# Softmax mixers and indexer in blocks of 16 meta tokens and 128 tokens, a search for the 16 lowest scores in the short block, and keys and indexer first in the weight stream

## The chip, the cores and the metric

The kernel runs on one core of one Trainium2 chip. The metric is the device time of one execution in microseconds (us), where lower is better. The kernel before takes 1382.4 us (median of 3 runs, 1382.38 to 1383.15).

## The reference, cut to what matters

The reference is two layers of a decoder trunk with D = 1024. 16 learned meta tokens stand ahead of 512 tokens, and are dropped at the end. All is in float32. A layer is

```
a    = rms_norm(h)
proj = a @ w_in                      # columns: dq dk dv iq iw ik | fq fk fv ff | gq gk gv gg lr
# DSA: 4 heads, one shared key; an indexer with 4 heads picks the keys of each query
score = sum_h iw[q,h] * relu(iq[q,h] . ik[k]) / 8, admissible keys only (k <= q)
sel   = top_k(score, 128)            # ties go to the earlier key
o_a   = softmax over sel of (rope(norm(dq)) . rope(norm(dk)) / 8) @ dv
# FoX: 4 heads, softmax attention with a forget gate (cumulated log-sigmoid) in the logits
# GLA: 4 heads, gated linear attention in chunks, RMS norm and SiLU gate on its output
h = h + concat(o_a, o_b, o_c) @ w_out
h = h + (silu(f @ w_gate) * (f @ w_up)) @ w_down,   f = rms_norm(h)
```

A query picks 128 keys. Among the first 144 tokens (16 meta tokens and 128 tokens) at most 16 keys are left out.

## The kernel before, in words

**Weights.** All weights come as a stream of units of 128 output columns by 1024 rows, 100 loads for each layer: 24 of the input projection, 8 of the output projection, 44 of gate and up, 24 of down. SyncE loads a unit into one of two buffers `raw` (L697), ScalarE rounds it to `whi` (L1187, "round"), GpSimd takes the rest `wlo = raw - whi` (L727, "split"), and TensorE multiplies with three products of the parts (whi x xhi, whi x xlo, wlo x xhi). Unit n+2 can be rounded only when TensorE is done with unit n. `DQ, DKIK, IQ, SMALL, FQ, ...` (top of the file) give each unit its number in the stream: units 0 and 1 are the queries of DSA, 2 is its key together with the indexer's key, 3 and 4 are the indexer's queries, 5 (`SMALL`) holds dv, the indexer's weights iw and the small gates.

**Tokens.** 528 tokens are 5 blocks of BLK = 106 (`NB`), 530 with two padded. Softmax mixers, indexer and GLA all use these blocks. A DSA or FoX head of block i works on (i + 1) * 106 keys: `logits` (TensorE L1012, then VectorE L1607: mask, negate and minimum in one pass, then ScalarE L1337: exp), `turn` (TensorE transposes L1021, ScalarE copy L1345), `values` (TensorE L1035), and for 4 heads together `scale` (VectorE L1618, L1619), `back` (TensorE L1044) and `mixed` (ScalarE L1376, VectorE L1628), which write the block's part of the output projection's input. The ten groups of four heads go in `ATTEND_ORDER`, which begins with the two groups of block 0. Both layers do all ten.

**The choice of keys.** For blocks 1 to 4 the indexer computes `index` (TensorE L992, ScalarE relu L1328, VectorE weighted sum L1571 and L1573, and after the fourth head the causal mask L1578). Then `topk` runs 16 rounds on VectorE, each one MAX8 (the 8 largest, L1585) and a match and replace (two instructions, L1586) over all keys of the block; `select` (L1591, L1592) turns the marks into a mask. The DSA logits of block i wait for it. The first `index` on TensorE waits for all five rotary units (`ROPE_ORDER`), the copies of the keys and `clear_keys` on GpSimd.

**GLA and the end of the mixers.** GLA's output is normed, gated and split on VectorE and ScalarE (L1666, L1671, L1381, L1676). `out` part 0 multiplies the GLA half of the first output units once all four `gla_lo` (L1676) are there; part 1 adds the attention half once the last `mixed` is done. After that the rest of the layer, which is output projection and FFN, is one long stream of units.

**The order of the work.** In the projection and mixer stage a planner (`plan`, `work`) writes out one static order for each engine. It has a cost table for each step, what each step waits for, and a list of priorities for each chain of steps (`BIAS`, one dict per layer). It fills TensorE between mixer steps with thirds of projection units. Each engine then runs its list in order. A step that waits holds up what stands behind it on that engine. In layer 1 the units made for queries only are computed for the 512 tokens alone. A layer's first two units go ahead of the list in `first_halves`.

Of the kernel before, what the change touches and what calls it, by code (L numbers as in the profile page):

```python
# [15 lines left out]
NB = 5  # L16
# [5 lines left out]
CUT = NT // 2  # L22
KT = D // 128
FF = 2816
MF = FF // 128
TOPK = 128
# [6 lines left out]
DQ, DKIK, IQ, SMALL, FQ, FK, FV, GQ, GK, GV, GG = 0, 2, 3, 5, 6, 8, 10, 12, 14, 16, 20  # L33
# [16 lines left out]
C_TRI = C_CAU + BLK  # L50
# [14 lines left out]
NORMED = {0: P_DQ, 1: P_DQ, 2: P_DK, 6: P_FQ, 7: P_FQ, 8: P_FK, 9: P_FK}  # L65
ROPED = (0, 1, 2, 3, 4)
# [3 lines left out]
ATTEND_ORDER = [(0, 0), (1, 0), (0, 1), (1, 4), (0, 2), (1, 3), (0, 3), (1, 2), (0, 4), (1, 1)]  # L70

# [33 lines left out]

HEADS = [(g, i, h) for g, i in ATTEND_ORDER for h in range(4)]
NORM_ORDER = [DQ, DQ + 1, DKIK, FQ, FQ + 1, FK, FK + 1] + [GV + h for h in range(4)]
ROPE_ORDER = (DKIK, DQ, DQ + 1, IQ, IQ + 1)
# [5 lines left out]
def chains_of_steps(l):  # L114

    choose = []
    for i in range(1, NB):
        choose += [("topk", i, r) for r in range(TOPK // 8)] + [("select", i)]
# [8 lines left out]
        "index": [("index", i, h) for i in range(1, NB) for h in range(4)],  # L127
# [10 lines left out]
        "logits": [("logits", *h) for h in HEADS],  # L138
        "turn": [("turn", *h) for h in HEADS],
        "values": [("values", *h) for h in HEADS],  # L140
        "scale": [("scale", *a) for a in ATTEND_ORDER],
        "back": [("back", *a) for a in ATTEND_ORDER],
        "mixed": [("mixed", *a) for a in ATTEND_ORDER],
# [7 lines left out]
def work(l, step):  # L151
# [4 lines left out]
    if kind in ("index", "topk", "select"):  # L156
        keys = (a[0] + 1) * BLK
    elif kind in ("logits", "turn", "values"):
        keys = (a[1] + 1) * BLK
# [60 lines left out]
    if kind == "clear_keys":  # L220
        return [(POOLE, 2.1, [(("proj", 3, 1, PIECES - 1), POOLE)])]
# [12 lines left out]
    if kind == "index":  # L234
        i, h = a
        n = 4 * (i - 1) + h
        cut = [min(keys, 512)] + ([keys - 512] if keys > 512 else [])
        used = [(("index", (n - 2) // 4 + 1, (n - 2) % 4), DVEE)] if n >= 2 else []
        return [(PE, sum(pe_fp32(c) for c in cut), ropes + [(("copies",), ACTE), (("clear_keys",), POOLE)]),
                (ACTE, act_us(keys, True), used),  # L240
                (DVEE, dve_us(keys, h > 0) + (0.3 if h == 3 else 0),
                 [turned(SMALL)] + ([(("logits", 0, i - 2, 3), DVEE)] if i >= 3 else []))]
    if kind == "topk":
        return [(DVEE, 0.46 + keys / 480, [(("index", a[0], 3), DVEE)])]
    if kind == "select":
        i = a[0]
        return [(DVEE, 0.6 + keys / 960, [])]
    if kind == "logits":
        g, i, h = a
        u = HEADS.index(a)  # L250
# [3 lines left out]
        before = [(("turn", *HEADS[u - 3]), PE)] if u >= 3 else []  # L254
# [3 lines left out]
    if kind == "turn":  # L258
        u = HEADS.index(a)
        return [(PE, 0.091 * (a[1] + 1), [(("logits", *a), ACTE)]),  # L260
                (ACTE, act_us(keys, True), [(("values", *HEADS[u - 2]), PE)] if u >= 2 else [])]
    if kind == "values":
        g, i, h = a
        n = ATTEND_ORDER.index((g, i))
        return [(PE, 0.186 * (i + 1), [(("turn", *a), ACTE)] + [turned(t) for t in ((FV, FV + 1) if g else (SMALL,))] +
                 ([(("scale", *ATTEND_ORDER[n - 1]), DVEE)] if h == 0 and n else []))]
    if kind == "scale":
        n = ATTEND_ORDER.index(a)
        return [(DVEE, 0.62, [(("values", *a, 3), PE)] + ([(("back", *ATTEND_ORDER[n - 1]), PE)] if n else []))]
# [25 lines left out]
    if kind == "out":  # L295
        if a[0] == 0:
            return [(PE, 4.4, [(("gla_lo", h), DVEE) for h in range(4)] + [evicted(N_PROJ - 1)])]
        return [(PE, 1.5, [(("mixed", *x), DVEE) for x in ATTEND_ORDER])]
# [10 lines left out]
def width_of(job):  # L309
    block = job[1] if job[0] == "index" else job[2] if job[0] in ("logits", "turn") else 0  # L310
    return 2 if job[0] in WIDE_KINDS or (block + 1) * BLK > 512 else 1
# [44 lines left out]
def tails(l, chains):  # L356
# [33 lines left out]
    for key in ops:  # L390
# [4 lines left out]
BIAS = ({'gla_lo': -60.8, 'prenorm': -39.5, 'turn': 91.9, 'gla_att': -2.6, 'norm': 26.4, 'gla_out': 147.1, 'mixed': -2.9, 'square': 15.1, 'gate': 4.2, 'fox': -28.5, 'out': 1.3, 'index': -23.6, 'gla_mix': -64.4, 'silu': -26.6, 'choose': -112.9, 'back': 49.6, 'proj': -40.9, 'scale': 56.4, 'gla_kv': -4.2, 'values': -16.4, 'turn_tile': -5.1},  # L395
        {'gla_lo': -34.5, 'prenorm': 40.0, 'copies': 16.5, 'clears': -85.6, 'gla_att': -2.9, 'logits': -10.1, 'norm': 78.2, 'gla_out': 174.3, 'mixed': 55.0, 'square': 5.1, 'gate': 5.6, 'fox': 6.6, 'out': -170.7, 'index': -19.4, 'gla_mix': -47.0, 'silu': 68.1, 'choose': -52.0, 'back': -18.0, 'proj': -38.1, 'rope': 4.4, 'scale': 82.1, 'turn_tile': 34.1, 'values': 8.4})
# [3 lines left out]
def plan(l, bias=None, start=9.0):  # L400
# [5 lines left out]
    info, drains = {}, {("back",) + a: [(("spread_sums",), POOLE)] + [(("gate", t), PE) for t in range(2)] for a in ATTEND_ORDER}  # L406
# [82 lines left out]
LOGITS = {s: n for n, s in enumerate(HEADS)}  # L489
GROUPS = {s: n for n, s in enumerate(ATTEND_ORDER)}  # L490
BACKS = GROUPS
ROPES = {k: n for n, k in enumerate(ROPE_ORDER)}
INDEX = {(i, h): 4 * (i - 1) + h for i in range(1, NB) for h in range(4)}
# [58 lines left out]
def hybrid_block(nc, hT, weights, params, consts, out):  # L552
    with ExitStack() as ctx:
# [18 lines left out]
        with ExitStack() as mixers:  # L572
# [1255 lines left out]
```

## Time and profile before

| | |
|---|---|
| median of 3 runs | 1382.4 us |
| the profiled execution's own time | 1382.82 us |
| its span in the profile | 1381.0 us |
| TensorE (PE) busy | 1356.4 us, 98% |
| VectorE (DVE) busy | 672.1 us, 49% |
| ScalarE (ACT) busy | 503.4 us, 36% |
| GpSimd (POOL) busy | 531.8 us, 39% |
| DMA | 112.46 MB, mean 81 GB/s |

The page gives an engine's busy time as the union of its instructions. TensorE's matmuls overlap, and their ends are modelled, so a gap on TensorE is a little longer than the profile shows it. The mixer stage of layer 0 is about 14 to 271 us, that of layer 1 about 715 to 961 us. The rest is the output projection and the FFN.

### The profile page before, as it was taken

What the parts mean: (1) busy time and instruction counts of PE and PEld (TensorE: products, weight loads), DVE (VectorE), ACT (ScalarE), POOL (GpSimd) and SP (SyncE); (2) the same over time, 40 slices, a digit from 0 to 9 for tenths busy, and PEclk for the clock granted to TensorE, in tenths of its full rate; (3) what the DMA queues carried; (4) which work ended last, traced back from release to release, by engine and by line L of the source; (5) the groups of instructions that cost most, each with busy time, mean ns of one, the idle gap of its engine ahead of it and who ended that gap; (6) DMA issues with size and microseconds to landing.
All of it is one profiled execution on the core that took longest, in us unless ns stands there. A gap on an engine that the chain in (4) does not pass through costs nothing.

```text
span 1381.0 us, 23323 instructions
## 1 busy us (share of the span) xinstructions
PE 1356.4 (98%) x8908; PEld 1221.5 (88%) x8908; DVE 672.1 (49%) x1174; ACT 503.4 (36%) x745; POOL 531.8 (39%) x248
## 2 busy tenths in 40 slices
PE   7999999999999999999999999999999999999998
PEld 7999889899999999999988988787878888888887
DVE  4669888654333333322235789895543333332000
ACT  5344545533222222322233553446332232223122
POOL 2553110243444444444436532111444444444444
PEclk9999999999999999999999999999999999999999
DMA  4221100122222222223222121011222332223234
GB/s 182 77 77 62 48 31 1 62 76 92 87 84 88 90 91 91 92 92 107 91 83 86 63 76 47 17 47 31 77 92 91 96 101 91 91 91 107 96 102 152
DMA packets 32170, 112.46 MB, mean 81 GB/s; under 512 B 3696, under 2 KB 4080, under 8 KB 31984
## 3 DMA queue, kind: packets, MB, share of 16 engines
q1 hardware_dynamic: 31392, 110.58, 24.3%
q10 hardware_dynamic: 720, 1.09, 0.2%
q8 instruction: 39, 0.64, 0.2%
q14 instruction: 19, 0.16, 0.0%
HBM read 109.55 MB, written 2.10 MB: 81 GB/s over the span
## 4 chain that ended last, share of the span: by engine, by line
PE 57%; issue 30%; POOL 8%; DVE 4%; ACT 1%; POOLq 0%; DMA 0%; SPq 0%; DVEq 0%; ACTq 0%
PE ps L837 19%; PE ps L843 9%; POOL wlo L727 8%; PE ps L933 5%; PE ps L927 5%; PE ps L928 5%; PE ps L1012 2%; PE ps L1035 2%; PE ps L941 1%; PE ps L992 1%; PE ps L1021 1%; PE ps L968 1%; DVE feat L1552 1%; PE ps L951 1%; PE ps L1076 1%
## 5 line engine op out<-in xcount | busy, mean ns | idle before, releaser
L727 POOL TENSOR_TENSOR wlo<-raw,whi 128x1024 fp32r<-128x1024 f32 x202 | 501.1, 2481 | 832.1 <-ACT whi L1187 831.9
L1187 ACT ACTIVATE whi<-raw 128x1024 fp32r<-128x1024 f32 x202 | 213.7, 1058 | 597.0 <-PE ps L843 559.9
L837 PE MATMUL ps<-xhi,whi 128*128 128x264 f32 (+1 forms) x1088 | 327.2, 323 | 7.2 <-ACT whi L1187 7.1
L837 PE MATMUL ps<-xlo,whi 128*128 128x264 f32 (+1 forms) x1088 | 325.7, 323 | 0.0
L837 PEld LDWEIGHTS ps<-xhi,whi 128*128 128x128 f32 x1088 | 205.3, 189 | 24.8 <-ACT whi L1187 6.8
L837 PEld LDWEIGHTS ps<-xlo,whi 128*128 128x128 f32 x1088 | 205.2, 189 | 16.4
L843 PE MATMUL ps<-xhi,wlo 128*128 128x264 f32 (+1 forms) x1088 | 195.3, 322 | 0.4 <-POOL wlo L727 0.2
L927 PE MATMUL ps<-xhi,whi 128*128 128x264 f32 (+1 forms) x640 | 181.7, 314 | 1.0 <-DVE feat L1473 1.0
L843 PEld LDWEIGHTS ps<-xhi,wlo 128*128 128x128 f32 x1088 | 162.4, 188 | 17.7 <-issue 1.0
L928 PE MATMUL ps<-xlo,whi 128*128 128x264 f32 (+1 forms) x640 | 171.8, 298 | 0.0
L837 PE MATMUL ps<-hhi,whi 128*128 128x264 f32 (+1 forms) x528 | 157.0, 320 | 0.0
L837 PE MATMUL ps<-hlo,whi 128*128 128x264 f32 (+1 forms) x528 | 156.9, 320 | 0.0
L1704 DVE TENSOR_TENSOR hid<-ps,rstd 128x528 f32<-128x528 f32 (+1 forms) x44 | 30.8, 700 | 213.1 <-PE ps L843 213.1
L927 PEld LDWEIGHTS ps<-xhi,whi 128*128 128x128 f32 x640 | 120.6, 188 | 6.7 <-DVE feat L1473 1.2
L928 PEld LDWEIGHTS ps<-xlo,whi 128*128 128x128 f32 x640 | 120.7, 189 | 4.7 <-issue 0.7
L1719 DVE TENSOR_TENSOR h<-ps,h 128x528 f32<-128x528 f32 (+1 forms) x16 | 11.2, 700 | 204.1 <-PE ps L843 204.1
L837 PEld LDWEIGHTS ps<-hhi,whi 128*128 128x128 f32 x528 | 99.3, 188 | 7.7
L837 PEld LDWEIGHTS ps<-hlo,whi 128*128 128x128 f32 x528 | 99.2, 188 | 7.6
L933 PE MATMUL ps<-xhi,wlo 128*128 128x264 f32 (+1 forms) x640 | 105.0, 306 | 0.3 <-POOL wlo L727 0.3
L1710 DVE TENSOR_TENSOR hlo<-hid,hhi 128x528 f32 (+1 forms) x44 | 82.9, 1885 | 41.0 <-ACT hhi L1410 41.0
L843 PE MATMUL ps<-hhi,wlo 128*128 128x264 f32 (+1 forms) x528 | 95.6, 321 | 0.0
L933 PEld LDWEIGHTS ps<-xhi,wlo 128*128 128x128 f32 x640 | 88.2, 188 | 5.3 <-issue 1.0
(154 smaller groups left out, 1742.0 us busy)
## 6 DMA issues: line engine op xcount, KB each, us to landing
raw<-in_weights SPq DMA_DIRECT2D x202, 512.0 KB, 3.5
out_hT<-h SPq DMA_DIRECT2D x8, 256.0 KB, 4.3
h<-in_hT SPq DMA_DIRECT2D x4, 264.0 KB, 6.3
h<-in_hT ACTq DMA_DIRECT2D x4, 264.0 KB, 5.8
cst<-in_consts SPq DMA_DIRECT2D x1, 1035.0 KB, 9.7
par_all<-in_params SPq DMA_DIRECT2D x1, 144.0 KB, 9.4
par_all<-in_params SPq DMA_DIRECT2D x1, 140.0 KB, 9.5
cst<-in_consts SPq DMA_DIRECT2D x1, 128.0 KB, 4.8
```

Of the source, the lines that this page charges most:

```text
L727: nc.gpsimd.tensor_tensor(wlo[:, b], raw[:, b], whi[:, b].bitcast(F32), ALU.subtract).then_inc(split_done, 1)
L837: nc.tensor.matmul(bank(bank_no, cut.stop - cut.start), whi[:, b, k % KT], x(k)[t][:, cut], start=(first and k == ks[0] and t == 0), stop= ...
L843: ins = nc.tensor.matmul(bank(bank_no, cut.stop - cut.start), wlo[:, b, k % KT], x(k)[0][:, cut], start=False, stop=(last and k == ks[-1]))
L927: nc.tensor.matmul(o, whi[:, k % 2, n], xhi[:, n, cut], start=(n == 0), stop=False)
L928: nc.tensor.matmul(o, whi[:, k % 2, n], xlo[:, n, cut], start=False, stop=False)
L933: ins = nc.tensor.matmul(o, wlo[:, k % 2, n], xhi[:, n, cut], start=False, stop=(n == KT - 1))
L941: ins = nc.tensor.matmul(bank(b0 + hf, HALF), lhs, sqb[:, SQUARES[k] % 2, hf * HALF:(hf + 1) * HALF], start=True, stop=True)
L1012: ins = nc.tensor.matmul(ps[0:BLK, b0 * 512 + a:b0 * 512 + z], q, key[:, a:z], start=True, stop=True)
L1035: ins = nc.tensor.matmul(ps[0:BLK, 3 * 512 + hd * 65:3 * 512 + (hd + 1) * 65], probs_t[:, u % 2, j, :], v, start=(j == 0), stop=(j == i))
L1187: return nc.scalar.activation(whi[:, b], raw[:, b], ACT.Copy).then_inc(hi_done, 1)
L1704: nc.vector.tensor_tensor(tokens(l, hid[:, b]), wide(l, 4 * b + 2), tokens(l, rstd[:]), ALU.mult).then_inc(ev.acc_free, 1)
L1710: nc.vector.tensor_tensor(hlo[:, bass.ds(j * 2 + b, 1), of].rearrange("p a t -> p (a t)"), hid[:, b, of], hhi[:, bass.ds(j * 2 + b, 1), of ...
```

## The change

It does five things.

1. The softmax mixers and the indexer take query blocks and key blocks of 16 meta tokens (block 0) and then 128 tokens each (blocks 1 to 4), with 16, 144, 272, 400 and 528 keys. GLA keeps its blocks of 106.
2. In the last layer the two attention groups of block 0, the meta tokens' queries, are left out, as the output drops them.
3. Block 1, with 144 keys, does not look for the 128 highest scores. The scores are negated with the causal mask in the same instruction, and `lowest` finds the 16 highest of these (MAX8, match and replace, MAX8). `select` then marks the scores at the sixteenth value or beyond and treats ties by a running count. The mask has the same meaning as before.
4. The stream begins with the keys (DKIK), the indexer's queries (IQ) and SMALL, and the DSA queries (DQ) follow as units 4 and 5. The first `index` waits for three rotary units, not five; `clear_keys` on GpSimd may come after unit 1, not unit 3; VectorE's first weighted sum waits for `masks` on GpSimd. In layer 1 `first_halves` takes three halves (both of DKIK, and IQ).
5. The planner's costs and its priorities `BIAS` are new, so all engines' lists in the mixer stage are new.

```
-DQ, DKIK, IQ, SMALL, FQ, FK, FV, GQ, GK, GV, GG = 0, 2, 3, 5, 6, 8, 10, 12, 14, 16, 20
+DKIK, IQ, SMALL, DQ, FQ, FK, FV, GQ, GK, GV, GG = 0, 1, 3, 4, 6, 8, 10, 12, 14, 16, 20
+QB = 128
+NQ = 1 + SEQ // QB
+def keys_to(i):
+    return META + QB * i
+def tokens_of(i):
+    return slice(keys_to(i - 1) if i else 0, keys_to(i))
+def rows_of(i):
+    return slice(0, QB if i else META)
-HEADS = [(g, i, h) for g, i in ATTEND_ORDER for h in range(4)]
-ROPE_ORDER = (DKIK, DQ, DQ + 1, IQ, IQ + 1)
+ATTENDED = [[(g, i) for g, i in ATTEND_ORDER if i or l < DEPTH - 1] for l in range(DEPTH)]
+HEADS = [[(g, i, h) for g, i in ATTENDED[l] for h in range(4)] for l in range(DEPTH)]
+ROPE_ORDER = (DKIK, IQ, IQ + 1, DQ, DQ + 1)
+INDEX_ROPES = 3
...
-    for i in range(1, NB):
-        choose += [("topk", i, r) for r in range(TOPK // 8)] + [("select", i)]
+    for i in range(1, NQ):
+        choose += [("lowest", i)] if keys_to(i) - TOPK <= 16 else [("topk", i, r) for r in range(TOPK // 8)]
+        choose += [("select", i)]
...
     if kind == "clear_keys":
-        return [(POOLE, 2.1, [(("proj", 3, 1, PIECES - 1), POOLE)])]
+        return [(POOLE, 2.1, [(("proj", 1, 1, PIECES - 1), POOLE)])]
...
                 def first_halves():
-                    halves_now = proj_halves(l)[:2]
+                    halves_now = proj_halves(l)[:3 if l else 2]
...
                 def index(i, hd):            # TensorE
-                        pe.wait_ge(ev.roped, len(ROPES))
+                        pe.wait_ge(ev.roped, INDEX_ROPES)
...
                 def index(i, hd):            # VectorE
                     if n == 0:
...
+                        dve.wait_ge(ev.masks_ready, 5)
...
-                    if hd == 3:
+                    if hd == 3 and nk - TOPK <= 16:
+                        chain(nc.vector.scalar_tensor_tensor(sc, sc, -1.0, causal_to(nk), ALU.mult, ALU.subtract))
+                    elif hd == 3:
...
+                def lowest(i):
+                    nk = keys_to(i)
+                    sc, rest = score[:, i % 2, 0:nk], score[:, i % 2, nk:2 * nk]
+                    chain(nc.vector.max(top8[:, 0:8], sc))
+                    chain(nc.vector.match_replace(out=rest, in_to_replace=top8[:, 0:8], in_values=sc, imm_value=TAKEN))
+                    chain(nc.vector.max(top8[:, 8:16], rest))
                 def select(i):
+                    if nk - TOPK <= 16:
+                        eq, cum = score[:, i % 2, nk:2 * nk], score[:, i % 2, 2 * nk:3 * nk]
+                        edge, among = top8[:, nk - TOPK - 1:nk - TOPK], top8[:, 16:17]
+                        chain(nc.vector.tensor_scalar(eq, sc, edge, None, ALU.is_equal))
+                        chain(nc.vector.tensor_tensor_scan(cum, eq, eq, 0.0, ALU.add, ALU.max))
+                        same = score[:, i % 2, 3 * nk:4 * nk - TOPK]
+                        chain(nc.vector.tensor_scalar(same, top8[:, 0:nk - TOPK], edge, None, ALU.is_equal))
+                        chain(nc.vector.tensor_reduce(among, same, AX.X, ALU.add))
+                        chain(nc.vector.tensor_tensor(among, cum[:, nk - 1:nk], among, ALU.subtract))
+                        chain(nc.vector.scalar_tensor_tensor(cum, cum, among, eq, ALU.is_gt, ALU.mult))
+                        chain(nc.vector.scalar_tensor_tensor(sc, sc, edge, cum, ALU.is_gt, ALU.add))
+                        nc.vector.scalar_tensor_tensor(sc, sc, NEG, causal_to(nk), ALU.mult, ALU.add).then_inc(ev.selected, 1)
...
                 def values(g, i, hd):
                     for j in range(i + 1):
-                        v = v_dsa[:, j] if g == 0 else v_fox[:, j, hd]
-                        ins = nc.tensor.matmul(ps[0:BLK, 3 * 512 + hd * 65:3 * 512 + (hd + 1) * 65],
-                                               probs_t[:, u % 2, j, :], v, start=(j == 0), stop=(j == i))
+                        keys, queries = rows_of(j), rows_of(i)
+                        v = v_dsa[keys, j] if g == 0 else v_fox[keys, j, hd]
+                        ins = nc.tensor.matmul(ps[queries, 3 * 512 + hd * 65:3 * 512 + (hd + 1) * 65],
+                                               probs_t[keys, u % 2, j, queries], v, start=(j == 0), stop=(j == i))
```

## Rows read from the trace of the kernel before

**Rows 1.** The page: busy time by engine.
```profile
PE 1356.4 (98%) x8908; PEld 1221.5 (88%) x8908; DVE 672.1 (49%) x1174; ACT 503.4 (36%) x745; POOL 531.8 (39%) x248
```

**Rows 2.** Busy time by stage: stretch, length, PE, PEld, DVE, ACT, POOL busy, granted clock, DMA.
```profile
14.00:85.00 71.00, 70.85 (x526) 68.12 (x525) 36.65 (x50) 28.12 (x41) 37.05 (x29) 1.00 0.22 75
85.00:250.00 165.00, 161.99 (x1263) 148.07 (x1262) 147.08 (x378) 82.14 (x152) 35.09 (x15) 1.00 0.14 45
250.00:271.00 21.00, 18.01 (x137) 14.63 (x136) 14.83 (x34) 13.82 (x27) 5.09 (x2) 0.99 0.17 58
271.00:290.00 19.00, 19.00 (x147) 19.00 (x147) 7.94 (x9) 4.55 (x7) 4.80 (x2) 0.92 0.16 49
715.00:760.00 45.00, 43.41 (x235) 37.05 (x235) 23.94 (x29) 17.94 (x25) 23.50 (x18) 1.00 0.21 71
760.00:941.00 181.00, 177.73 (x1242) 156.59 (x1241) 154.14 (x379) 89.65 (x164) 46.48 (x26) 1.00 0.15 48
941.00:961.50 20.50, 18.22 (x127) 13.62 (x126) 15.03 (x35) 13.73 (x28) 4.74 (x2) 0.97 0.17 52
961.50:980.00 18.50, 18.50 (x70) 14.85 (x71) 7.28 (x6) 3.48 (x5) 4.87 (x2) 0.85 0.08 28
```

**Rows 3.** Timeline, end of layer 0's mixers: start, us, work [idle before, who released it].
```profile
269.83 0.70 DVE L1676 TENSOR_TENSOR mix_lo<-feat,mix_hi 128x532 fp32r<-128x532 f32 x1
270.06 0.37 PE L1044 MATMUL ps<-cst,o_tok 106*128 106x106 f32 x2 [0.89 <-DVE o_tok L1619]
...
271.78 0.42 PE L837 MATMUL ps<-mix_lo,whi 128*128 128x264 f32 x1
...
274.42 0.29 PE L837 MATMUL ps<-mix_hi,whi 128*128 128x264 f32 x1
```

**Rows 4.** Chain that ended last, 183 to 207 us: start, time until the next step, what.
```profile
186.56 0.71 PE ps L1012 x2
...
188.25 0.97 PE ps L992 x4
...
193.03 0.36 PE ps L1021 x4
193.39 0.71 PE ps L1035 x8
...
206.14 0.22 PE ps L1076 x2
```

**Rows 5.** Groups by line and shape on VectorE: count | busy us, mean ns of one | idle before.
```profile
L1585 DVE MAX8 top<-score 106x8 f32<-106x530 f32 x32 | 22.7, 708 | 0.4
...
L1585 DVE MAX8 top<-score 106x8 f32<-106x212 f32 x32 | 12.1, 378 | 0.6
L1586 DVE MATCH_VALUE_LOAD score<-top,score 106x8 f32 x128 | 11.8, 92 | 4.4
L1586 DVE MATCH_REPLACE8 score<-top,score 106x212 f32<-106x212 f32 x32 | 11.6, 364 | 0.0
...
L1522 DVE TENSOR_TENSOR_SCAN feat<-cst,feat 128x532 f32<-128x532 f32 x4 | 9.2, 2301 | 0.1
...
L1528 DVE TENSOR_TENSOR coef<-coef,feat 128x8 f32<-128x8 f32 x2 | 0.4, 176 | 0.1
```

**Rows 6.** Timeline of VectorE: end of the last rotary unit, first score, last search.
```profile
59.67 0.71 DVE L1513 TENSOR_TENSOR feat<-xnb 128x532 f32<-128x532 f32 x1
...
85.31 0.33 DVE L1571 TENSOR_SCALAR score<-relu,w_idx 106x212 f32<-106x212 f32 x1
...
248.91 0.44 DVE L1591 TENSOR_SCALAR score<-score 106x530 f32<-106x530 f32 x1
```

**Rows 7.** Timeline of POOL, layer 0: clears and masks between two weight splits.
```profile
38.51 2.39 POOL L727 TENSOR_TENSOR wlo<-raw,whi 128x1024 fp32r<-128x1024 f32 x1 [4.11 <-ACT whi L1187]
...
46.93 2.03 POOL L754 MEMSET kk<- 64x1064 f32 x2
...
54.21 1.30 POOL L746 COPY q_odd<-cst 4x532 f32<-4x532 f32 x2
```

More of the change, by code:

```diff
@@ L126, in chains_of_steps @@
         "turn_tile": [("turn_tile", k) for k in (SMALL, FV, FV + 1, GV, GV + 1, GV + 2, GV + 3)],
-        "index": [("index", i, h) for i in range(1, NB) for h in range(4)],
+        "index": [("index", i, h) for i in range(1, NQ) for h in range(4)],
         "choose": choose,
@@ L137, in chains_of_steps @@
         "gla_lo": [("gla_lo", h) for h in range(4)],
[L138 to L143, printed above, removed]
+        "logits": [("logits", *h) for h in HEADS[l]],
+        "turn": [("turn", *h) for h in HEADS[l]],
+        "values": [("values", *h) for h in HEADS[l]],
+        "scale": [("scale", *a) for a in ATTENDED[l]],
+        "back": [("back", *a) for a in ATTENDED[l]],
+        "mixed": [("mixed", *a) for a in ATTENDED[l]],
         "out": [("out", p) for p in range(2)],
@@ L238, in work @@
         used = [(("index", (n - 2) // 4 + 1, (n - 2) % 4), DVEE)] if n >= 2 else []
-        return [(PE, sum(pe_fp32(c) for c in cut), ropes + [(("copies",), ACTE), (("clear_keys",), POOLE)]),
+        return [(PE, sum(pe_fp32(c) for c in cut), ropes[:INDEX_ROPES] + [(("copies",), ACTE), (("clear_keys",), POOLE)]),
                 (ACTE, act_us(keys, True), used),
                 (DVEE, dve_us(keys, h > 0) + (0.3 if h == 3 else 0),
-                 [turned(SMALL)] + ([(("logits", 0, i - 2, 3), DVEE)] if i >= 3 else []))]
+                 [turned(SMALL), (("masks",), POOLE)] + ([(("logits", 0, i - 2, 3), DVEE)] if i >= 3 else []))]
+    if kind == "lowest":
+        return [(DVEE, 3 * (0.16 + keys / 960) + 0.1, [(("index", a[0], 3), DVEE)])]
     if kind == "topk":
@@ L258, in work @@
     if kind == "turn":
-        u = HEADS.index(a)
-        return [(PE, 0.091 * (a[1] + 1), [(("logits", *a), ACTE)]),
-                (ACTE, act_us(keys, True), [(("values", *HEADS[u - 2]), PE)] if u >= 2 else [])]
+        u = HEADS[l].index(a)
+        return [(PE, 0.109 * (a[1] + 1) if a[1] else 0.06, [(("logits", *a), ACTE)]),
+                (ACTE, act_us(QB * (a[1] + 1), True), [(("values", *HEADS[l][u - 2]), PE)] if u >= 2 else [])]
     if kind == "values":
         g, i, h = a
-        n = ATTEND_ORDER.index((g, i))
-        return [(PE, 0.186 * (i + 1), [(("turn", *a), ACTE)] + [turned(t) for t in ((FV, FV + 1) if g else (SMALL,))] +
-                 ([(("scale", *ATTEND_ORDER[n - 1]), DVEE)] if h == 0 and n else []))]
+        n = ATTENDED[l].index((g, i))
+        return [(PE, 0.225 * (i + 1) if i else 0.12, [(("turn", *a), ACTE)] + [turned(t) for t in ((FV, FV + 1) if g else (SMALL,))] +
+                 ([(("scale", *ATTENDED[l][n - 1]), DVEE)] if h == 0 and n else []))]
     if kind == "scale":
-        n = ATTEND_ORDER.index(a)
-        return [(DVEE, 0.62, [(("values", *a, 3), PE)] + ([(("back", *ATTEND_ORDER[n - 1]), PE)] if n else []))]
+        n = ATTENDED[l].index(a)
+        return [(DVEE, 0.62, [(("values", *a, 3), PE)] + ([(("back", *ATTENDED[l][n - 1]), PE)] if n else []))]
     if kind == "back":
@@ L405, in plan @@
     todo = {}
-    info, drains = {}, {("back",) + a: [(("spread_sums",), POOLE)] + [(("gate", t), PE) for t in range(2)] for a in ATTEND_ORDER}
+    info, drains = {}, {("back",) + a: [(("spread_sums",), POOLE)] + [(("gate", t), PE) for t in range(2)] for a in ATTENDED[l]}
     for name, chain in chains.items():
@@ L488 @@
 NORMS = SQUARES
-LOGITS = {s: n for n, s in enumerate(HEADS)}
-GROUPS = {s: n for n, s in enumerate(ATTEND_ORDER)}
-BACKS = GROUPS
+LOGITS = [{s: n for n, s in enumerate(heads)} for heads in HEADS]
+GROUPS = [{s: n for n, s in enumerate(groups)} for groups in ATTENDED]
 ROPES = {k: n for n, k in enumerate(ROPE_ORDER)}
-INDEX = {(i, h): 4 * (i - 1) + h for i in range(1, NB) for h in range(4)}
+INDEX = {(i, h): 4 * (i - 1) + h for i in range(1, NQ) for h in range(4)}
 def turn_of(l, job):
@@ L653, in group_waits @@
             last = {}
-            for s in BACKS:
+            for s in GROUPS[l]:
                 p, n = turn_of(l, ("back",) + s)
@@ L957, in turn_tile @@
                     pe.wait_ge(ev.feat_ready, 2 * k + 2)
-                    turn_blocks(feat[:, place(k), :], b0, done)
+                    if k >= GV:
+                        turn_blocks(feat[:, place(k), :], b0, done)
+                        return
+                    for i in range(NQ):
+                        col = b0 * 512 + i * 128
+                        of = tokens_of(i) if i else slice(0, QB)
+                        ins = nc.tensor.transpose(ps[:, col:col + 128], feat[:, place(k), of], ident)
+                    ins.then_inc(done, 1)
                 def turn_k(t):
```

193 lines of the change are left out of this document (102 added, 91 removed).

## The prediction, made before the change was run

> **What bounds the kernel now.** I read the page first. TensorE is busy 98% of the span, no other engine over 49% [rows 1], and its clock is at the upper level (2.4 GHz, a granted clock of 1.00) in all stretches but the ends of the two mixer stages [rows 2]. So a change pays only by what it takes off TensorE's own work, or off the places where TensorE is not full. The change touches the two mixer stages alone. For them I read the table by stage next [rows 2]. In the middle of layer 0's stage (85 to 250 us) VectorE is busy 147.08 of 165 us, and in layer 1's (760 to 941) 154.14 of 181. TensorE still finds enough to do there, as the list fills it with projection work. It misses 165.00 - 161.99 = 3.0 us in layer 0, and 1.6 (715 to 760) + 3.3 = 4.9 us in layer 1.
>
> The ends of the stages look different. From 250 to 271 TensorE is busy 18.01 of 21.00 us, from 941 to 961.5 18.22 of 20.50: 3.0 and 2.3 us idle. The timeline shows why [rows 3]. The projections are used up, only attention is left, and each step waits for a VectorE result (0.89 us before the last back at 270.06); the last `gla_lo` (L1676) starts at 269.83, so `out` part 0, which could have covered the last wait, can't start before it. The last search ends only at 248.9 us [rows 6], and the four DSA heads of block 4 have to come after it. Behind these gaps the clock falls to its lower level, 1.2 GHz: the same 264-column matmuls are 0.42 us long at 271.78 and 0.29 at 274.42 [rows 3]. From the granted clock this costs 21 x 0.01 + 19 x 0.08 = 1.7 us in layer 0 and 20.5 x 0.03 + 18.5 x 0.15 = 3.4 us in layer 1 [rows 2]. **The two ends cost 3.0 + 1.7 + 2.3 + 3.4 = 10.4 us.** The mixer stage as a whole is bound by TensorE, its end by VectorE.
>
> **The change on VectorE.** Block 1's search is now 16 rounds of 378 + 92 + 364 ns = 13.3 us [rows 5], with two mask instructions of 0.3 us each by the formula that follows: 13.9 us a layer. The new one has 11 small instructions and one search mask in place of another. A VectorE instruction costs 176 ns at 8 elements and 708 at 530, so about 170 ns + 1.02 ns an element [rows 5]. At 144 elements: two MAX8 0.6 us, a match and replace 0.4, three passes with two inputs 0.37 each (1.0 ns an element), one compare 0.25 and three tiny ones 0.18 each; the scan by its own row is (2301 - 170)/532 = 4 ns an element, so 0.75. Sum 3.6, with the gaps between dependent ones 4.0 us. It saves 9.9 us. The 16 rounds of blocks 2 to 4 run over 46, 24 and 2 keys fewer: 16 x 2.07 x 72 ns = 2.4 us. `logits` has 230 keys fewer a head: 8 x 230 x 1.04 ns = 1.9 us, the weighted sums 0.6. **VectorE does 14.8 us less in layer 0**, and in layer 1 about 4 us less again, since eight reductions, two `scale` and two `mixed` of block 0 are gone. VectorE's groups have 106 or 128 rows alike, and I take rows as free.
>
> It also starts earlier. The last rotary unit ended at 60.4 us and the first score was summed only at 85.31 [rows 6]; VectorE was busy 36.65 of the first 71 us [rows 2], so there is room. Now three rotary units and `SMALL` as fourth unit suffice, two units (about 12 us of stream) sooner. So searches move from the full stretch into an empty one. With 15 to 19 us less to do, VectorE should be done with the last search well before TensorE is done with the projections: the tail, in which VectorE was 14.83 of 21 us busy, needs less than what is gained. The heads of block 4 then run between projection units and `gla_lo` comes before the last heads, so that `out` part 0 (36 matmuls of 0.12 us, 4.4 us) covers the last scale, back and mix. Of 10.4 us I leave 0.5 a layer: **-9.4 us**.
>
> **The change on TensorE.** The chain of waits gives the time from step to step in a full stretch [rows 4]: `logits` of a head with 424 keys 0.71 us, with 530 0.97 (`index` alike), so 1.67 ns a key; four transposes 0.36 (0.09 each); eight `values` instructions 0.71 (0.09 each). With 128 queries a block the price of the last two rises.
> - Transposes: 128 columns move, not 106, so 0.109 for 0.09; 14 a head (1 + ... + 5, less block 0) make 1.53, block 0 0.05, against 15 x 0.091 = 1.37. 8 heads: +1.7 us.
> - Values: 65 columns move either way. Two instructions of L1076, with 106 moving columns and 128 stationary ones, take 0.22, or 0.11 each, where L1021 with 106 and 106 takes 0.09 [rows 4]. The stationary columns set this step, so `values` rises from 0.093 to 0.111: per head 2.9 + 0.1 against 2.63, +3.0 us. The row it is nearest to is L1076; the lower bound is no rise at all, the upper one 2 x 14 x 0.018 x 8 = 4.0.
> - Logits: 16 to 528 keys make 2.35 + 0.12 (block 0, between 0.06 and 0.19) against 2.77: -2.5 us. Index: 4 x 0.235 = -0.9. Back: two instructions of 0.11 for 0.09 in ten groups, +0.3.
>
> Sum +1.6 us in layer 0. In layer 1 block 0's heads go as well (8 x 0.27 + 0.3 = 2.5): -0.9. **TensorE together +0.7 us**, bounds -5 and +3.
>
> The Trainium skill (TensorE: Matmul & The Clock Gate, Back-to-back issue gap) has a formula in which the gap goes by the moving columns alone; by it `values` would not rise, and the sum would be 6 us lower. The trace speaks against it: at 65 moving columns the step is 0.09 us, as with 106.
>
> **Waits in the middle.** TensorE's 7.9 us of gaps there hang on single long VectorE instructions and on the lists. The lists are all new, so such gaps come again in other places. With less VectorE work I take a third or more away: **-3 us**, between +3 and -7.
>
> **The new waits.** The first `index` stands behind three rotary units and `clear_keys` on TensorE's list, and projection units can be put ahead of it; VectorE's first weighted sum waits for the masks, and evictions of projection banks are queued behind it. POOL's clears take from 46.93 to 55.5 us with no split between them [rows 7]; in the first units POOL idles about 4 us between splits (4.11 before 38.51), so moving 4.5 us of them there makes one split up to 0.5 us late. ScalarE's copies of `turn` grow by 330 columns a head and its exps shrink by 230: nothing. Units, loads and their bytes are the same, and DQ's move changes no queue's length. In layer 1 IQ as third half waits for the last eviction of the layer before, while 14 matmuls of 0.12 us for each of the two halves of DKIK run: covered. I take **+0.5 us**, bounds 0 and +7.
>
> **Sum.** -9.4 + 0.7 - 3 + 0.5 = -11.2 us. The profiled execution took 1382.8, the median is 0.4 lower at 1382.4, so 1371.2 us. A measurement of this kernel can tell 0.2%, 2.8 us.
>
> **Rivals.**
> - *The ends stay half.* Search was not the only late thing: the two GLA instructions at the end and the chain of the last group stay, and the clock still falls once behind each gap. For it: `gla_lo` is VectorE work with its own order, and a gap of under 1 us stood just ahead of each fall. Against: VectorE has 15 us to give. Half of 10.4 stays, and middle gaps shrink by 1.5 only: 1382.4 - 5.2 + 0.7 - 1.5 + 0.5 = 1376.9. Chance 0.17.
> - *More is gone*: both ends whole (-10.4), the middle gaps mostly (-6), `values` at its lower bound (-3 of 6): 1382.4 - 10.4 - 6 - 2.3 = 1363.7. Chance 0.10.
> - *It doesn't come earlier.* The rotary units were ready at 60.4 and the sum came at 85.3, so the wait for five units was not what held the search. If the lists keep it there, only the shorter search is left, 15 us on VectorE, which still covers the tail: 1373, inside the forecast.
> - *Nothing.* The new lists put as much gap into the middle as the ends gave: 1382. Chance 0.07.
> - *Slower: the splits at the head of each layer.* All of POOL's clears (8.7 us) are pulled ahead with `clear_keys`, since the index waits for it. A split then is 8.7 - 4.1 = 4.6 us late, TensorE stands at a low pass with no mixer work to fill in so early, and the clock falls behind it (2 us): 6.6 us a layer, 13.2, against a gain of 11.2: 1384.4, with middle gaps that don't shrink 1387. It decides from 5.6 us a layer. For it: the first units have nothing beside them. Against: only two clears are needed early. Chance 0.08.
>
> **How the numbers follow.** The forecast has 0.58, and the time is its own: 1371.2. The range takes in the half case and the bounds on TensorE's work and middle gaps: 1364 to 1379; about 0.8 lies in it. Faster by over 2.8 us: 0.58 + 0.17 + 0.10 = 0.85; within 0.07; slower 0.08.
>
> **What would show it.** Right: TensorE full from 250 us to the output projection and in layer 1's end, no clock below 1.00 there; the last search over before the last projection unit is evicted; MAX8 of block 1 twice a layer and the first score before 75 us; the step of `values` at 0.11. The first matmul of the output stage comes about 5 us earlier in layer 0, and the span is 11 us shorter, with the FFN stretches unchanged. Wrong: gaps as long at the ends with another releaser (ACT or `gla_lo`), a split late in the first 60 us with idle TensorE beside it, or more than 8 us of gaps in the middle.

## The result, and the profile after

The changed kernel takes 1406.05 us (median of 4 runs, 1404.95 to 1408.46), the kernel before beside it 1382.39 us (4 runs). The ratio is 1.0174, with a 95% interval of 1.0156 to 1.0191: **slower by 23.7 us**, where 11.2 us less were forecast, and far outside the range of 1364 to 1379. The profiled execution took 1405.7 us, with a span of 1403.9 us.

The page, busy time by engine:

```profile
PE 1381.5 (98%) x8864; PEld 1234.3 (88%) x8864; DVE 646.1 (46%) x1076; ACT 498.8 (36%) x727; POOL 529.2 (38%) x248
```

Against [rows 1], VectorE is 26.0 us less busy, as meant. TensorE runs 44 instructions fewer and is busy 25.1 us longer. So the time was not lost in idle stretches. The table by stage says the same (stretch, length, busy time of PE, PEld, DVE, ACT and POOL, granted clock, DMA share, GB/s); the stages end later now, so the stretches do too:

```profile
7.00:85.00 78.00, 77.43 (x547) 73.20 (x548) 43.91 (x64) 33.66 (x53) 35.10 (x25) 1.00 0.30 106
85.00:262.00 177.00, 175.86 (x1275) 154.87 (x1274) 130.78 (x332) 81.21 (x150) 41.88 (x22) 1.00 0.14 46
262.00:283.00 21.00, 20.24 (x128) 16.34 (x127) 13.06 (x33) 14.16 (x27) 2.35 (x1) 0.93 0.09 26
283.00:302.00 19.00, 17.98 (x133) 17.77 (x133) 7.83 (x9) 4.85 (x7) 4.81 (x2) 0.89 0.09 29
...
770.00:962.00 192.00, 186.83 (x1195) 160.97 (x1195) 159.33 (x339) 86.82 (x148) 46.41 (x26) 0.99 0.14 47
962.00:984.00 22.00, 20.65 (x136) 16.48 (x135) 13.81 (x33) 14.44 (x28) 2.36 (x1) 0.99 0.08 25
984.00:1002.00 18.00, 16.98 (x69) 13.51 (x68) 7.11 (x7) 3.64 (x5) 4.83 (x2) 0.92 0.09 29
```

In the middle of layer 0 VectorE now has slack (130.78 of 177 us, where it was 147.08 of 165 [rows 2]) and TensorE is idle for 1.14 us instead of 3.0. And yet the first matmul of the output projection starts at 282.5 us instead of 270.6, and in layer 1 at 983.1 instead of 961.3. TensorE's mixer work itself takes longer. The chain of waits (start, time until the next step, what) shows where, in a full stretch of layer 0:

```profile
185.26 0.55 PE ps L1054 x5
185.81 0.46 PE ps L1042 x2
186.27 1.40 PE ps L1069 x10
187.67 0.34 PE ps L1054 x3
...
192.53 0.58 PE ps L998 x5
193.11 0.95 PE ps L1069 x6
```

L1054 is `turn`: 0.11 us a transpose, as forecast. L1069 is `values`; a key block is two records there. A head with five key blocks takes 1.40 us, that is 0.140 a record, and one with three takes 0.95, or 0.158. Forecast were 0.111 for either, and the old kernel needed 0.71 for eight [rows 4]. The fewer key blocks a head has, the dearer each seems, so something is paid **once a head**. What is new in every head is one key block of 16 rows. The groups of that line by shape don't show it (`16*128 16x65` is 16 contraction rows, 128 stationary columns, 65 moving columns; then count | busy us, mean ns of one | idle before):

```profile
L1069 PE MATMUL ps<-v_fox,probs_t 128*128 128x65 f32 x160 | 25.2, 289 | 0.0
L1069 PE MATMUL ps<-v_fox,probs_t 16*128 16x65 f32 x64 | 14.3, 304 | 0.0
L1069 PEld LDWEIGHTS ps<-v_fox,probs_t 128*128 128x128 f32 x160 | 20.7, 193 | 2.3
L1069 PEld LDWEIGHTS ps<-v_fox,probs_t 16*128 16x128 f32 x64 | 9.8, 190 | 5.4 <-issue 4.8
```

The durations of single instructions are nearly equal: 289 and 304 ns for the matmuls, 193 and 190 ns for the weight loads (PEld). The Trainium skill (TensorE: Matmul & The Clock Gate, LDWEIGHTS) says that a weight load takes as long with 32 rows as with 128; the 190 ns with 16 rows and 193 ns with 128 here agree. Only the last column of the weight loads differs, 5.4 against 2.3 us idle, and it has no releaser but "issue". The starts show it plainly. In the head whose first `values` record is at 169.21 us, the steps from start to start are 0.193 into the first record of 16 rows, 0.161 to the second, 0.200 to the first of 128 rows, 0.161 to the next, and 0.112 from there on. Four steps cost 0.08, 0.05, 0.09 and 0.05 more than 0.11, some 0.27 us in all; with the step behind full rows, which is often shorter than 0.11, it is 0.33 a head in the comparison below.

The old trace had one place of this kind, which the prediction did not read: `gate` of GLA (L977 in the kernel before) contracts over 16 rows. The chain of waits of the kernel before, 107 to 110 us:

```profile
107.22 0.12 PE ps L928
107.34 1.99 PE ps L977 x8
109.33 0.32 PE ps L927
```

The `L927` step is 0.12 us everywhere else in that stretch. Behind the 16-row instructions it is 0.32.

### The profile page after: what moved, and what is told of

Its sections match the earlier page's. It is cut to its first block, busy times and chain, and to the rows that moved or that the text cites. A ratio compares the mean times of both kernels' runs of the same rounds, so it can differ in the third digit from the quotient of the medians.

```text
span 1403.9 us, 23076 instructions
## 1 busy us (share of the span) xinstructions
PE 1381.5 (98%) x8864; PEld 1234.3 (88%) x8864; DVE 646.1 (46%) x1076; ACT 498.8 (36%) x727; POOL 529.2 (38%) x248
## 3 DMA queue, kind: packets, MB, share of 16 engines
q1 hardware_dynamic: 31392, 110.59, 23.7%
q10 hardware_dynamic: 720, 1.09, 0.2%
## 4 chain that ended last, share of the span: by engine, by line
PE 54%; issue 32%; POOL 8%; DVE 4%; ACT 1%; DMA 0%; POOLq 0%; SPq 0%; DVEq 0%; ACTq 0%
PE ps L859 19%; PE ps L865 9%; POOL wlo L749 8%; PE ps L949 5%; PE ps L950 5%; PE ps L955 5%; PE ps L1069 2%; PE ps L1042 2%; PE ps L1054 1%; PE ps L963 1%; PE ps L1022 1%; PE ps L973 1%; DVE score L1615 1%; PE ps L915 1%; PE ps L1093 1%
## 5 line engine op out<-in xcount | busy, mean ns | idle before, releaser
L1789 DVE TENSOR_TENSOR h<-ps,h 128x528 f32<-128x528 f32 (+1 forms) x16 | 11.2, 700 | 204.3 <-PE ps L865 204.3
```

## The experiments

**1. Full rows (a_full).** The whole change is kept; only `values` goes over all 128 rows of key block 0. For this POOL clears the rows of `v_dsa` and `v_fox` beyond 16 once, and ScalarE copies block 0's 16 rows of v by an instruction of their own (10 instructions more), so that the zeros stay. Block 0's own heads keep their 16 rows.

```
-                        keys, queries = rows_of(j), rows_of(i)
+                        keys, queries = rows_of(i), rows_of(i)
...
+                    nc.gpsimd.memset(v_dsa[:, 0], 0.0).then_inc(ev.masks_ready, 1)
+                    pool.wait_ge(ev.masks_ready, 6)
+                    nc.gpsimd.memset(v_fox[:, 0], 0.0).then_inc(ev.masks_ready, 1)
...
```

> The kernel after, with values on full rows: block 0's keys are multiplied with all 128 rows, the rows behind the 16 meta tokens being zero in v. Same lists, same number of matmuls. Theory A (a TensorE instruction with 16 rows costs extra each time the rows change: +0.09 us into it, +0.05 between the pair, +0.09 out of it, 64 heads): about 15 us faster than the kernel after, 1391 us. Theory B (the new lists and their waits are what costs): it stays at 1404 to 1406 us.

Measured: 1381.51 us (10 runs, 1379.68 to 1382.46), ratio to the kernel before 0.9994 (0.9985 to 1.0004). That is **24.5 us less than the change as it stood**, all of its loss, and 10 us more than was expected of it: the expectation had 0.23 us a head and did not count the second step behind the 16 rows, nor the clock. TensorE executes the same 8864 instructions. Its stages (columns as above):

```profile
85.00:251.00 166.00, 164.84 (x1247) 150.56 (x1245) 128.15 (x328) 78.04 (x148) 41.92 (x22) 1.00 0.16 49
251.00:272.00 21.00, 20.24 (x153) 17.53 (x152) 15.37 (x34) 17.23 (x32) 2.37 (x1) 1.00 0.08 26
272.00:291.00 19.00, 17.97 (x148) 17.77 (x148) 8.71 (x10) 4.85 (x7) 4.82 (x2) 1.00 0.13 36
715.00:760.00 45.00, 45.00 (x231) 38.00 (x231) 11.95 (x16) 16.77 (x24) 25.33 (x23) 1.00 0.25 81
760.00:939.00 179.00, 173.48 (x1168) 154.28 (x1167) 153.00 (x330) 85.84 (x150) 46.36 (x25) 1.00 0.15 50
939.00:959.70 20.70, 20.03 (x151) 17.41 (x150) 14.58 (x38) 14.88 (x29) 2.50 (x1) 1.00 0.08 26
959.70:980.00 20.30, 19.28 (x84) 15.41 (x83) 9.46 (x10) 6.45 (x9) 6.00 (x3) 1.00 0.16 52
```

Its chain of waits at the same place (`values` is L1076 there):

```profile
187.20 1.06 PE ps L1076 x10
...
190.97 0.62 PE ps L1076 x6
```

1.40 became 1.06 and 0.95 became 0.62: 0.33 us a head. 64 heads (blocks 1 to 4, two groups of four, two layers) make 21.1 us. Summed over the trace, the steps of `values` with the step into each head fall from 81.7 to 60.5 us, by 21.2. The rest of the 24.5, 3.3 us, was not taken apart. It is less than what the falls of the clock come to in the changed kernel (7.2 us in the account below), and a_full has none: the granted clock is 1.00 in every stretch here.

**2. The price by itself (b_extra16 and b_extra106).** In the kernel *before*, with its own lists of work, each head gets one more instruction on key block 0. One kernel uses 16 rows, the other all 106 (so those keys count twice).

```
+                        if j == 0:
+                            few = slice(0, META)        # b_extra106: slice(0, BLK)
+                            v = v_dsa[few, j] if g == 0 else v_fox[few, j, hd]
+                            ins = nc.tensor.matmul(ps[0:BLK, 3 * 512 + hd * 65:3 * 512 + (hd + 1) * 65],
+                                                   probs_t[few, u % 2, j, :], v, start=False, stop=(i == 0))
```

> The same as b_extra106 but the added pair takes 16 rows alone (so keys 0 to 15 count twice). Theory A: each pair costs 0.23 us more than with 106 rows, 80 pairs: 18 us over b_extra106, 1410 to 1416 us. Theory B: the same time as b_extra106 within 2 us.

> The kernel before, with one more pair of matmuls in each of the 80 value steps, block 0's keys once more with all 106 rows (so block 0's keys count twice). Control for the next run. 160 instructions of 0.093 us: +15 us at most, 1392 to 1398 us.

Measured: 1415.64 us (ratio 1.0242, 1.0222 to 1.0263) with 16 rows, 1392.59 us (1.0076, 1.0055 to 1.0096) with 106. 80 heads, so (1415.64 - 1392.59)/80 = 0.29 us for one change to 16 rows and back, which for itself does *less* arithmetic. The 23.1 us are above the 18 that were expected, for the same reason as above. The two chains of waits, a head with three key blocks in each; first 16 rows:

```profile
186.46 0.15 PE ps L1035 x2
186.61 0.33 PE ps L1040 x2
186.94 0.52 PE ps L1035 x4
187.45 0.27 PE ps L1021 x3
```

then 106 rows:

```profile
185.51 0.15 PE ps L1035 x2
185.67 0.19 PE ps L1040 x2
185.85 0.37 PE ps L1035 x4
186.23 0.27 PE ps L1021 x3
```

L1040 is the added instruction: 0.33 against 0.19, and behind it, back on 106 rows, 0.52 against 0.37. Each is 0.14 to 0.15 more, 0.29 together, the 0.29 of the times. The steps of these lines sum to 94.4 and 72.7 us in the two traces, 21.7 of the 23.1 us. So this price needs neither the new lists nor the shapes of 128 nor the short search, since none of them is in these kernels.

**3. The order of the stream alone (b_stream).** The kernel before with the new order of units, the index after three rotary units, the earlier clears and three first halves in layer 1; old priorities.

```
-DQ, DKIK, IQ, SMALL, FQ, FK, FV, GQ, GK, GV, GG = 0, 2, 3, 5, 6, 8, 10, 12, 14, 16, 20
+DKIK, IQ, SMALL, DQ, FQ, FK, FV, GQ, GK, GV, GG = 0, 1, 3, 4, 6, 8, 10, 12, 14, 16, 20
...
+INDEX_ROPES = 3
```

> The kernel before with the stream order of the change alone (keys and indexer first, three rotary units before the first index, three first halves in layer 1), old blocks, old search, old priorities. Theory A: TensorE's work is the same, so within 5 us of the kernel before, either way. Theory B (the new order at the head of the layer makes waits): 1392 us or more, with the gaps in the first 60 us of a layer.

Measured: 1391.6 us (2 runs, 1390.06 and 1393.14), ratio 1.0068 (1.0048 to 1.0089). That fits no expectation well. The head of each layer is not slow, as the rival of the splits would have it; layer 0's mixers take what they took (264.7 us against 263.8, from the layer's first matmul to the first of the output projection). Layer 1's take 263.0 against 253.8, with 11.4 us of gaps in them where it was 7.1, and with the granted clock at 0.50 from 956.2 for 20.5 us at their end. The priorities were fitted to the other order, so this run says what the order does to an unfitted list, and not what the order is worth.

**4. The parts of the change, undone one at a time from a_full.** Each gets new lists by the same priorities, and the cuts show only the line that decides. The short search back to 16 rounds (a_full_topk), the old order of the stream (a_full_stream), and block 0's groups of the last layer kept (a_full_keep0):

```
-        choose += [("lowest", i)] if keys_to(i) - TOPK <= 16 else [("topk", i, r) for r in range(TOPK // 8)]
+        choose += [("lowest", i)] if keys_to(i) - TOPK <= 0 else [("topk", i, r) for r in range(TOPK // 8)]
```

> The kernel with values on full rows, its short search undone: block 1 takes the 16 rounds of MAX8 and match and replace over 144 keys again. The planner writes new lists with the same priorities. VectorE gets 16 x 0.72 = 11.5 us of work back for about 4 us. If VectorE bounds the mixer stages, up to 7 us a layer slower (1389 to 1396 us); if TensorE does, within 3 us of the run with the short search (1379 to 1385 us).

```
-DKIK, IQ, SMALL, DQ, FQ, FK, FV, GQ, GK, GV, GG = 0, 1, 3, 4, 6, 8, 10, 12, 14, 16, 20
+DQ, DKIK, IQ, SMALL, FQ, FK, FV, GQ, GK, GV, GG = 0, 2, 3, 5, 6, 8, 10, 12, 14, 16, 20
...
-                    halves_now = proj_halves(l)[:3 if l else 2]
+                    halves_now = proj_halves(l)[:2]
```

> The kernel with values on full rows, its stream order undone (DQ first again, five rotary units before the first index, two first halves). New lists with the same priorities. If an earlier start of the searches is what pays, 3 to 8 us slower, 1385 to 1390 us; if not, within 3 us of 1381.5 us.

```
-ATTENDED = [[(g, i) for g, i in ATTEND_ORDER if i or l < DEPTH - 1] for l in range(DEPTH)]
+ATTENDED = [[(g, i) for g, i in ATTEND_ORDER ] for l in range(DEPTH)]
```

> The kernel with values on full rows, but layer 1 does the two attention groups of block 0 again. TensorE's work rises by 2.5 us by my count, and this block's 16-row instructions come back in 8 heads (about 1.5 us): 1384 to 1387 us. If what was left out was hidden anyway: 1381.5 us.

Measured, beside 1381.51 us of a_full:

| undone | us (runs) | ratio to the kernel before | VectorE busy |
|---|---|---|---|
| short search | 1379.93 (10) | 0.9984 (0.9975 to 0.9994) | 660.4 |
| order of the stream | 1382.81 (10) | 1.0007 (0.9998 to 1.0016) | 638.1 |
| block 0 left out in layer 1 | 1395.7 (4) | 1.0099 (1.0084 to 1.0115) | 644.0 |

The short search takes 17.9 us off VectorE (660.4 to 642.5) and nothing off the time; without it the median is 1.6 us lower, inside the spread of the runs. The order of the stream is worth 1.3 us, less than the runs of one kernel differ among themselves (2.8 us in a_full). Keeping block 0's groups costs 14.2 us, where 2.5 to 5.5 were expected. By the steps in its trace only about 4 of these are their work; the others are gaps and two falls of the clock (at 822.9 and 979.9 us, 3.4 us each at 0.50). That a list fitted to this kernel would avoid them is likely and not shown: none was fitted. With b_stream, 9.4 us over the kernel before, it says that an unfitted list can cost more than any of these parts brings.

**5. No instruction of 16 rows at all (a_best), and its priorities fitted anew.** The gate of GLA, block 0's own `turn`, `values` and `back` go over 128 rows as well, over cleared memory; block 0's transposes become plain matmuls for it (12 TensorE records more). The lists stay.

```
-                        ins = nc.tensor.matmul(bank(b0 + hf, HALF), par[rows, P_W2 + t * 128:P_W2 + (t + 1) * 128],
-                                               feat[rows, place(SMALL), hf * HALF:(hf + 1) * HALF], start=True, stop=True)
+                        ins = nc.tensor.matmul(bank(b0 + hf, HALF), par[:, P_W2 + t * 128:P_W2 + (t + 1) * 128],
+                                               feat[:, place(SMALL), hf * HALF:(hf + 1) * HALF], start=True, stop=True)
...
-                        keys, queries = rows_of(i), rows_of(i)
+                        keys, queries = slice(0, QB), rows_of(i)
```

> The kernel with values on full rows, and the last 16-row instructions gone too: the GLA gate multiplies all 128 rows of SMALL with weights that are zero outside its 16 rows, and block 0's turn, values and back take 128 rows over memory that is cleared once. Lists unchanged. Theory A: 4 pairs of changes for the gates (0.18 us each) and 8 heads and two backs of block 0 with about 0.2 us each: 2 to 3 us faster than 1381.5 us, 1379 us. If only the 64 heads mattered: no change.

Measured: 1379.78 us (11 runs, 1378.34 to 1380.81), ratio 0.9983 (0.9974 to 0.9992). **This beats both kernels**, the changed one by 26.3 us and the one before by 2.5 us, which is little but outside the interval. Beside a_full (1381.51) it is 1.7 us; the two intervals overlap, but the sum of TensorE's steps falls by 1.6 us between the two traces (a step over 0.7 counted as 0.7), and 1.5 of these are the steps of `gate` with the one into each run of four.

`gate` also tells whether few rows are dear or the *change* of rows is. Two instructions, four records, stand in a row there, and the same four records are in both traces, first a_full with 16 rows, then a_best with 128:

```profile
121.89 0.28 PE L957 MATMUL ps<-xlo,whi 128*128 128x264 f32 x1
122.10 1.16 PE L1014 MATMUL ps<-feat,par_all 16*128 16x266 f32 x4
123.19 0.66 PE L994 MATMUL ps<-cst,feat 128*128 128x128 f32 x4
```

```profile
121.43 0.28 PE L960 MATMUL ps<-xlo,whi 128*128 128x264 f32 x1
121.55 1.06 PE L1016 MATMUL ps<-feat,par_all 128*128 128x266 f32 x4
122.45 0.60 PE L997 MATMUL ps<-cst,feat 128*128 128x128 f32 x4
```

The step into the four is 0.21 against 0.12 us, the four take 1.09 against 0.90. From start to start, the first of the four takes 0.328 against 0.225, the second and third 0.224 to 0.228 in both, the last 0.311 against 0.223, and the one behind it 0.167 against 0.109. So the price stands at the two borders, two steps at each, 0.34 us in all, and nothing is paid inside the run. And it is not paid at every change: GLA's output changes between 128 rows (L1109) and 106 rows (L1111) in the changed kernel, between 220.2 and 221.7 us seven times, and each step is 0.11 us, as without a change.

> The kernel with no 16-row instruction left, and its short search undone (16 rounds over 144 keys, new lists, same priorities). With values on full rows alone this undoing went from 1381.5 to 1379.9 us. If the short search really costs (its long dependent chain ahead of layer 1's first group), 1378 us; if that step was chance of the lists, 1379 to 1381 us.

a_best with the 16 rounds back (the edit of a_full_topk): 1380.28 us (11 runs), ratio 0.9985 (0.9976 to 0.9994). The two can't be told apart, so the sign of the short search stays open and its size is under 2 us either way.

> As a_best_topk, with the priorities and the order of the attention groups fitted anew in both layers (layer 1 begins with (0,1), (0,2), (0,3)). Work on TensorE is the same, only gaps can change: about 12 us of stalls over 0.4 us are left to win. If the lists' gaps are what holds these kernels, 1374 to 1378 us; if the planner's costs are not good enough to tell lists apart, 1378 to 1384 us.

a_best_topk with a new order of groups and new priorities (`ATTENDED` and both dicts of `BIAS`), searched with the kernel's own planner: 1383.76 us (11 runs, 1382.59 to 1386.11), ratio 1.0011 (1.0002 to 1.0020). The hope of 1374 to 1378 failed: the list that the planner's costs favour is 3.5 us slower than the one it was to replace. Those costs don't rank lists this close to each other.

## Why the prediction was wrong, step by step

**The step that failed is the price of `values` on TensorE.** The prediction said "The stationary columns set this step, so `values` rises from 0.093 to 0.111", and counted the key block of 16 rows like any other, in the +3.0 us of layer 0 and with no term for the change of rows. For full rows that was right: the steps are 0.112 us in the trace. The formula of the Trainium skill (TensorE: Matmul & The Clock Gate, Back-to-back issue gap) goes by the moving columns and gave no rise; the section gives it for an isolated matmul, and says that in a stream the weight load and the matmul set the spacing together. The second is what this trace agrees with, as the step rose with the stationary columns. But the nearest row for the *new shape*, a contraction over 16 rows, was not L1021 or L1076 [rows 4]; it was `gate`, L977, the one 16-row instruction, with its late successor. The upper bound of 3 us on TensorE's work rested on that oversight. Measured, the change to 16 rows and back costs 0.33 us a head, 21 us together; full rows in its place give back 24.5.

The other terms can be read against a_full, where that price is gone. TensorE's attention functions, as sums of the steps from each record's start to the next one's, up to the end of the last head (a step over 0.7 us, which is a wait, counted as 0.25; the columns are rounded):

| us | layer 0: before | after | a_full | layer 1: before | after | a_full |
|---|---|---|---|---|---|---|
| values | 21.8 | 33.5 | 25.5 | 21.9 | 31.1 | 23.9 |
| logits | 21.2 | 21.3 | 20.2 | 21.7 | 19.6 | 18.6 |
| turn | 11.5 | 13.1 | 12.8 | 12.3 | 13.3 | 12.3 |
| index | 8.8 | 9.5 | 9.3 | 9.1 | 8.0 | 8.0 |
| `turn_blocks` and its like | 4.4 | 4.9 | 4.7 | 4.6 | 4.6 | 4.5 |
| back | 2.3 | 2.7 | 2.4 | 2.2 | 2.3 | 1.9 |
| sum | 70.1 | 84.9 | 74.8 | 71.8 | 79.0 | 69.1 |

- *TensorE's work*, forecast +0.7: it is +21.9 in the changed kernel, nearly the whole 22.8 us between the two profiled executions. In a_full it is +4.7 in layer 0 (forecast +1.6) and -2.7 in layer 1 (forecast -0.9), so +2.0. `values` was to rise by 3.0 in layer 0 (by the prediction's own steps, 28 x 0.111 + 0.1 against 30 x 0.093 a head, it would be 3.3) and rose by 3.7, `turn` 1.3 for 1.7. `logits` fell by 1.0 where 2.5 were counted: this sum takes in short waits. Sizes off by about a microsecond, within the bounds.
- *VectorE*, forecast -14.8 us in layer 0 and -19 in layer 1: over both -26.0 us on the page, -29.6 in a_full. In the changed kernel the first score is summed at 74.49 us and the last search is over at 241.9, where it was 85.31 and 248.9 [rows 6]. So searches did come earlier, and VectorE did get its slack. This rival ("it doesn't come earlier") is out.
- *The ends*, forecast -9.4 of 10.4. In the changed kernel the idle time is 0.76 + 1.02 us in layer 0 and 1.35 + 1.02 in layer 1, and the clock, from the granted shares, costs 21 x 0.07 + 19 x 0.11 = 3.6 us and 22 x 0.01 + 18 x 0.08 = 1.7. With 1.9 us for a new fall in layer 1's middle (192 x 0.01, a rounded share) the clock cost 7.2 us, where it cost 5.1. In a_full the clock never falls, and idle are 0.76 + 1.03 and 0.67 + 1.02, so 3.5 us are left of 10.4: -6.9. The step that was too good is "`out` part 0 covers the last scale, back and mix": it comes before the last back now, but one wait of 1.0 us each stays behind it.
- *The middle gaps*, forecast -3 of 7.9: 1.14 + 5.17 us in the changed kernel, 1.16 + 5.52 in a_full. So -1.6 and -1.2. They did go elsewhere, as the prediction said. Of layer 1's, 2.8 us is one wait, behind the short search.
- *The rival on the slower side* (POOL's splits at the head of each layer): TensorE is idle for only 0.57 us from 7 to 85 and not at all from 715 to 770, so that mechanism did not occur. Its side was right and its reason was not; the case of the 16-row instructions, which did occur, was in no rival.

Of a_full's forecast parts that leaves -6.9 - 1.2 + 2.0 = -6.1 us, and 1382.8 - 6.1 = 1376.7. The profiled execution of a_full took 1380.2, its median is 1381.5. Some 3.5 us are spread over steps that I did not place: `gate` +0.2 and `rope` +0.3 in layer 0 are two that show. By layers, a_full gains nothing in layer 0, whose last matmul of the output projection starts at 320.4 us for 318.8. From the last matmul of layer 0's down projection to the last of layer 1's output projection it takes 296.2 us for 300.7. So all that the change gives, once its 16 rows are gone, is in the layer that leaves out block 0.

**What stays open**: by what mechanism TensorE pays for the change to 16 rows, and from how many rows on, as nothing between 16 and 106 was run; why the clock fell in the changed kernel at 280.2 us, for 6.8 us, with no gap longer than the 0.67 us that ended at 278.0 in the 16 us ahead of it; and how much of a_full's distance from 1371 is in its lists, since a fit that would settle it failed (refit_topk).

The wait behind the short search is the longest new one. TensorE's timeline, first the wait that stayed at the end of layer 0, then the one for the short search in layer 1 (start, us, work, idle before it and who released it):

```profile
290.43 0.36 PE L859 MATMUL ps<-mix_hi,whi 128*128 128x264 f32 x1 [1.02 <-DVE mix_lo L1698]
...
816.22 0.66 PE L1054 MATMUL ps<-cst,probs 128*128 128x128 f32 x2 [2.79 <-DVE stat L1677]
```

and VectorE's timeline ahead of the second:

```profile
807.89 3.64 DVE L1615 SCALAR_TENSOR_TENSOR score<-relu,w_idx,score 128x272 f32<-128x272 f32 x2
...
811.89 0.47 DVE L1648 TENSOR_SCALAR score<-score,top 128x144 f32<-128x144 f32 x1
812.40 0.87 DVE L1649 TENSOR_TENSOR_SCAN score<-score 128x144 f32<-128x144 f32 x1
813.30 0.42 DVE L1651 TENSOR_SCALAR score<-top 128x16 f32<-128x16 f32 x1
...
814.97 0.31 DVE L1656 SCALAR_TENSOR_TENSOR score<-score,causal 128x144 f32<-128x144 f32 x1
815.31 0.31 DVE L1677 CUSTOM_DVE_ANT_0 probs<-ps,score 128x144 f32<-128x144 f32 x1
```

In the last layer block 0 is left out, so block 1 is the first attention that TensorE can turn to, and it waits for this chain. The chain `select` takes 3.4 us (811.89 to 815.28), and two sums of block 2 (L1615) stand ahead of it with 3.64 us for two instructions of 272 elements, whose mean is 1.05 us over the kernel. The scan was forecast at 0.75 us and takes 0.87. Yet the short search is not what makes this wait. With the 16 rounds back (a_full_topk) it is still there:

```profile
806.41 0.41 PE L1061 MATMUL ps<-cst,probs 128*128 128x128 f32 x2 [2.23 <-DVE stat L1687]
```

Both kernels leave out block 0 in layer 1; that this makes the wait is argued and not shown. With block 0 kept (a_full_keep0) TensorE's longest wait in that layer's mixers is 1.9 us, at another line. Behind the gap of the changed kernel the clock is low: in the chain of waits two transposes take 0.43 us at 817.37, so 0.21 each, where they take 0.11 at 185.26.

## What to carry to other kernels

Don't put a float32 matmul of few contraction rows between full ones: where a block has 16 rows and its neighbours 128, clear the rest once and contract over all of them. Where it can't be filled up, put such matmuls side by side: a run of four records paid no more than a run of two. (106 rows beside 128 cost nothing here; what lies between 16 and 106 is not known.) When a change brings an instruction of a new shape, look in the old trace for the one instruction that already has it, and read the start-to-start steps around it, not its duration. Work taken off an engine that is not the bound is worth only the gaps that it held, here 18 us of VectorE for nothing that could be measured.

## What the runs showed of the hardware that was not expected

- A float32 matmul pair over 16 rows between pairs over 128 rows costs 0.33 us more than one over 128 rows in its place (0.29 between pairs over 106 rows), though its own duration and that of its weight load are the same. The step into the pair and the three behind it take 0.16 to 0.20 us each, where 0.11 is usual. A run of four 16-row records pays the same once, at its borders, and a change between 128 and 106 rows pays nothing. The idle time stands on the weight loads as "issue", with no releaser.
- The step of small float32 matmuls goes with the stationary columns: 0.093 us at 106 and 0.112 at 128, with 65 moving columns in both. It holds for a run of equals: behind a 512-column piece the 16 or 18 moving columns of the last keys take 0.03 us a record, with 128 or 106 stationary columns.
- Two VectorE instructions of 272 elements took 3.64 us where one of 144 takes 0.41 on average; they ran beside a weight split on POOL (2.5 and 1.1 us; the other four of that size, which at most touch a split, took 0.50 to 0.75). No run here took the split away, so this is not shown to be its cause.
